# Modulation weights of a two-layer block: products and sums on VectorE, one operation a tile

## The reference, cut to what matters

```python
# x: 512 tokens x 1024 features, f32. First block: two attentions (differential, latent), gated and merged
merged = sigmoid(g_diff) * (o_diff @ w_proj_diff) + sigmoid(g_mla) * (o_mla @ w_proj_mla)
x = rms_norm(x + merged @ w_out, norm_final)
# Second block: six vectors of 1024 features, the same for all tokens, shape the two sublayers
shift1, scale1, gate1, shift2, scale2, gate2 = split(silu(cond) @ mod_w + mod_b, 6)
h = rmsnorm(x, g1) * (1 + scale1) + shift1
x = x + gate1 * hyena_mix(h)            # long convolution by spectra
h = rmsnorm(x, g2) * (1 + scale2) + shift2
x = x + gate2 * conv_ffn(h)
out = rmsnorm(x, final_g)
```

## Time and profile before

| | us |
|---|---|
| runs, median of 3 | 1062.06 (1061.97 to 1062.47) |
| profiled execution | 1061.37 |
| its span, first to last instruction | 1059.3 |
| TensorE busy | 1040.0 |
| VectorE, ScalarE, GpSimd busy | 665.7, 418.6, 543.7 |

### The profile page before, as it was taken

How to read it: one execution, slowest core, us unless ns; L and a number is a source line. 1 busy time by engine, 2 the same in 40 slices (tenths; PEclk the granted TensorE clock), 3 DMA queues, 4 the chain that set the end, 5 groups by cost and what they waited for, 6 DMA issues and landing times.

```text
span 1059.3 us, 13471 instructions
## 1 busy us (share of the span) xinstructions
PE 1040.0 (98%) x4968; PEld 856.4 (81%) x4968; DVE 665.7 (63%) x1007; ACT 418.6 (40%) x687; POOL 543.7 (51%) x401
## 2 busy tenths in 40 slices
PE   7999999999999999999999999999999999999996
PEld 5889887877877888778888888778888888888885
DVE  5663776866499765985788847386666666520503
ACT  6223547665554243644444342442323223221222
POOL 1688895999200064234444346535465545553641
PEclk9999999999999999999999999999999999999999
DMA  6446454342446922212322113303222232223222
GB/s 257 164 168 225 133 187 153 90 163 70 179 159 238 379 104 100 93 67 80 110 83 84 54 42 155 143 33 146 87 80 79 103 135 79 80 80 135 104 80 79
DMA packets 19611, 131.92 MB, mean 125 GB/s; under 512 B 3411, under 2 KB 3811, under 8 KB 13030
## 3 DMA queue, kind: packets, MB, share of 16 engines
q1 hardware_dynamic: 8784, 92.62, 23.2%
q0 software_dynamic: 6560, 27.27, 8.0%
q10 hardware_dynamic: 4214, 11.30, 2.8%
HBM read 124.90 MB, written 6.30 MB: 124 GB/s over the span
## 4 chain that ended last, share of the span: by engine, by line
PE 95%; DVE 2%; ACT 1%; DMA 1%; issue 0%; POOL 0%; SPq 0%; POOLq 0%; ACTq 0%; DVEq 0%
PE bank L505 81%; PE bank L496 7%; PE bank L511 3%; PE bank L752 1%; PE bank L746 1%; DMA x_sb<-x_in 1%; PE bank L904 1%; PE bank L741 1%; DVE arena L2178 0%; DVE arena L2181 0%; PE bank L913 0%; PE bank L753 0%; PE bank L869 0%; ACT arena L1189 0%; DVE arena L2214 0%
## 5 line engine op out<-in xcount | busy, mean ns | idle before, releaser
L1730 POOL TENSOR_TENSOR ring_parts<-ring,ring_parts 128x1024 fp32r<-128x1024 f32 x102 | 248.7, 2442 | 266.3 <-ACT ring_parts L1189 263.5
L505 PE MATMUL bank<-hT_parts,ring_parts 128*128 128x512 f32 x1344 | 339.2, 393 | 0.8 <-ACT hT_parts L1518 0.8
L1189 ACT ACTIVATE ring_parts<-ring 128x1024 fp32r<-128x1024 f32 (+2 forms) x163 | 168.6, 1043 | 383.7 <-PE bank L505 219.9
L505 PEld LDWEIGHTS bank<-hT_parts,ring_parts 128*128 128x128 f32 x1344 | 249.6, 188 | 54.7 <-ACT hT_parts L1518 2.4
L505 PE MATMUL bank<-ring_parts,hT_parts 128*128 128x512 f32 (+1 forms) x672 | 171.6, 379 | 1.0 <-POOL ring_parts L1730 0.6
L505 PE MATMUL bank<-ring_parts,arena_parts 128*128 128x512 f32 (+1 forms) x736 | 172.4, 386 | 0.0
L505 PEld LDWEIGHTS bank<-ring_parts,arena_parts 128*128 128x128 f32 x736 | 136.6, 188 | 27.9 <-DVE arena L2416 0.3
L505 PE MATMUL bank<-arena_parts,ring_parts 128*128 128x512 f32 x592 | 148.0, 391 | 0.3 <-DVE arena_parts L2285 0.3
L505 PEld LDWEIGHTS bank<-ring_parts,hT_parts 128*128 128x128 f32 x672 | 122.4, 188 | 22.8 <-POOL ring_parts L1730 1.0
L2521 DVE SCALAR_TENSOR_TENSOR arena<-bank,small,arena 128x441 f32<-128x441 f32 (+2 forms) x176 | 122.3, 695 | 24.6 <-DVE arena L2521 1.7
L505 PEld LDWEIGHTS bank<-arena_parts,ring_parts 128*128 128x128 f32 x592 | 111.0, 188 | 25.4 <-DVE arena_parts L2285 2.1
(11 more groups left out here) (223 smaller groups left out, 1100.5 us busy)
## 6 DMA issues: line engine op xcount, KB each, us to landing
ring<-weights_in SPq DMA_DIRECT2D x39, 2048.0 KB, 8.0
arena<-mod_w_in POOLq DMA_DIRECT2D x32, 512.0 KB, 4.1
arena<-mod_w_in POOLq DMA_DIRECT2D x8, 1024.0 KB, 5.5
x_sb<-x_in SPq DMA_DIRECT2D x4, 512.0 KB, 5.7
ring<-weights_in SPq DMA_DIRECT2D x4, 512.0 KB, 8.5
mod_spill<-mod_part POOLq DMA_DIRECT2D x16, 128.0 KB, 2.1
x_sb<-x_in ACTq DMA_DIRECT2D x4, 512.0 KB, 12.2
arena<-mod_spill ACTq DMA_DIRECT2D x1, 2048.0 KB, 10.6
```

The source lines that it names most:

```text
L505: ins = nc.tensor.matmul(out, l, r, start=start and n == 0, stop=stop and n == len(passes) - 1)
L1189: return nc.scalar.activation(out, in_, ACT.Copy)
L1730: return nc.gpsimd.tensor_tensor(part(low), low, part(high), ALU.subtract)
```

## The change

The weights now come transposed: a tile has 128 output features on the partitions and all 1024 inputs on the columns. silu(cond) is a row that every partition holds (`cond_row`, in the first half of `mod_g`, by a transfer that spreads it and one Silu of 128x1024 behind split 8). One `scalar_tensor_tensor` on VectorE multiplies the tile with it and adds up along the columns into one column of `modc` (`mod_tile`): 48 tiles, 48 operations. Nothing is left for TensorE to add.

- 16 early tiles stand behind splits 12 to 23, through four buffers; 28 late tiles stand two by two behind splits `FIRST_GATE+6` to `FIRST_PD+3`, and four in the first half of the merge, again with four buffers. GpSimd only issues the loads, each waiting until the tile four places earlier is used, and takes the roots in between.
- `mod_spill`, `mod_back`, `ones_sq`, `modulation` and `gate_rows` on TensorE, the copies `modg_copy` and `modg_late`, and GpSimd's products are gone. VectorE's `modulation()` (bias, then 1 + scale times the norm's gain) moves from behind `norm_x2(3)` to before `add_wo(0)`.
- The gates are written as columns to HBM (`mod_row`), with a strided transfer from ScalarE's queue behind the last `square_x2`, and read back spread over all partitions.
- `small` grows by 8 columns, `modc` and the table `minus` lie ahead of the padding.

```diff
+        minus = sb("minus", [P, 256])
+        modc = sb("modc", [P, MOD_TILES])
         sb("to_line", [P, -((nc.sbuf_base + 31) // 32 * 32) % LINE // 4])
-        mod_part = sb("mod_part", [P, 2 * MOD_POOL_COLS])
-        modc = sb("modc", [P, 4 * KD])
...
+        cond_row = mod_g[:, 0, :]
+        modw_early = [at(99, D), at(103, D), at(65, D), mod_g[:, 1, :]]
+        modw_late = [at(75, D), at(79, D), at(65, D), at(69, D)]
...
-            modulation(0)
-            gate_rows(0)
             wo_tile(0)
             wo_tile(1)
-            modulation(1)
-            gate_rows(1)
             filter_tile(0)
             wo_tile(2)
-            modulation(2)
...
             wo_tile(7)
-            gate_rows(2)
-            gate_rows(3)
-            modulation(3)
...
+            chunk_landed(pool, C_DK)
+            pool.dma_start(cond_row, cond_d.partition_broadcast(P).rearrange("p a d -> p (a d)")).then_inc(sem("cond_in"), 16)
+            for j in range(MOD_EARLY):
+                load_mod(j)
+                if j == 11:
                     latent_roots()
+            for h in range(HEADS):
+                head_roots(h)
+            wait("o_ready", HEADS)
+            load_mod(MOD_EARLY)
+            load_mod(MOD_EARLY + 1)
+            wait("pv_done", 4 * UNITS)
+            for j in range(MOD_EARLY + 2, MOD_TILES):
+                load_mod(j)
...
+                V.scalar_tensor_tensor(out=w, in0=w, scalar=1.0, in1=cond_row, op0=ALU.mult, op1=ALU.mult,
+                                       accum_out=modc[:, j:j + 1]).then_inc(sem("mod_summed"), 1)
...
+                if i >= 4:
+                    mod_tile(i - 4)
-            for p in range(16, 24):
+            for p in range(16, 20):
                 split_low(p)
+                mod_tile(p - 12)
+            for p in range(20, 24):
+                split_low(p)
+                for j in range(2):
+                    mod_tile(8 + 2 * (p - 20) + j)
...
             for p in range(FIRST_GATE + 6, FIRST_PD + 4):
                 split_low(p)
+                for j in range(2):
+                    mod_tile(MOD_EARLY + 2 * (p - FIRST_GATE - 6) + j)
                 if p in (FIRST_GATE + 8, FIRST_GATE + 9):
                     split_output(p - FIRST_GATE + UNITS - 10)
                 if p - FIRST_GATE - 7 in NET_AFTER:
                     net_layer(NET_AFTER.index(p - FIRST_GATE - 7))
-                if p - FIRST_GATE in MOD_AFTER:
-                    mod_chunk(MOD_AFTER.index(p - FIRST_GATE))
...
+            wait("gates_ready", 1)
+            act.dma_start(mod_row_d.rearrange("a (t p) -> p (a t)", p=P), modc[:, 4 * KD:MOD_TILES],
+                          allow_slow_non_contiguous=True).then_inc(sem("mod_row_out"), 16)
```

More of the change, by code:

```diff
@@ L892, in _ @@
                          [(o[0][:, k, :], o[1][:, k, :]) for k in range(HEADS)]).then_inc(sem("merge_done"), 1)
[L895 to L914, removed]
             def abs_norm(n):
@@ L1256, in _ @@
                 split_high(p)
+                if p == 8:
+                    wait("cond_in", 16)
+                    nc.scalar.activation(cond_row, cond_row, ACT.Silu).then_inc(sem("cond_ready"), 1)
             for i in range(8, 12):
@@ L1951, in net_layer @@
                 wrap(r, a, k, 0).then_inc(sem("net_angle"), 1)
-            def mod_chunk(j):
-                C = MOD_DVE_COLS
-                wait(f"modw_in{j % 2}", 16 * (MOD_POOL // 2 + j // 2 + 1))
-                acc = mod_g[:].rearrange("p a b -> p (a b)")[:, j * C:(j + 1) * C]
-                w = modw_dve[j % 2]
-                for k in range(KD):
-                    ins = V.scalar_tensor_tensor(out=acc, in0=w[:, k, :], scalar=st(CSILU + k), in1=acc, op0=ALU.mult, op1=ALU.add)
-                    if k < KD - 1:
-                        link(ins)
-                ins.then_inc(sem("mod_dve_done"), 1)
             def table(t, m, groups, halves):
@@ L2107, in split_output, with modulation @@
                 V.tensor_tensor(part(low), low, part(high), ALU.subtract).then_inc(sem("oT_low"), 1)
+            def modulation():
+                wait("mod_summed", MOD_TILES)
+                V.tensor_tensor(modc[:], modc[:], small[:, SMALL["mod_b"]], ALU.add).then_inc(sem("gates_ready"), 1)
+                wait("gates_ready", 1)
+                for s, name in enumerate(("norm_g1", "norm_g2")):
+                    c = modc[:, (2 * s + 1) * KD:(2 * s + 2) * KD]
+                    ins = V.scalar_tensor_tensor(out=c, in0=c, scalar=1.0, in1=small[:, SMALL[name]], op0=ALU.add, op1=ALU.mult)
+                ins.then_inc(sem("modc_ready"), 1)
             wait("lambda_exps", 1)
@@ L2160, in _ @@
             split_low(FIRST_WO + 3)
-            def modulation():
-                wait("modc_done", 4)
-                V.tensor_tensor(modc[:], bank[3][:, 0:4 * KD], small[:, SMALL["mod_b"]], ALU.add).then_inc(sem("modc_read"), 1)
-                wait("modc_read", 1)
-                for s, name in enumerate(("norm_g1", "norm_g2")):
-                    c = modc[:, (2 * s + 1) * KD:(2 * s + 2) * KD]
-                    ins = V.scalar_tensor_tensor(out=c, in0=c, scalar=1.0, in1=small[:, SMALL[name]], op0=ALU.add, op1=ALU.mult)
-                ins.then_inc(sem("modc_ready"), 1)
+            modulation()
             def add_abs(i):
@@ L2480, in _ @@
             wait("row_in", 16)
[L2481 to L2482 removed]
+            wait("modg_in", 16)
             link(V.tensor_tensor(row[:], row[:], mod_g[:, 0, :], ALU.mult))
```

135 lines of the change are left out of this document (39 added, 96 removed).

## The result

| | before | after |
|---|---|---|
| median | 1062.01 us | 1068.01 us (1067.43 to 1068.58) |
| ratio, 95% interval | | 1.0056 (1.0044 to 1.0068) |
| profiled execution, its span | 1061.37, 1059.3 | 1067.97, 1066.2 |

The change makes the kernel 6 us slower, where 2 us less were forecast. The page of after shows what the earlier trace rows shows of before: the busy times, and the chain by engine.

What follows compares the result with a forecast made beforehand. TensorE, busy for 98% of the span, was taken to bound the kernel; -5.4 (of 10.4 us removed) + 2.9 (latent stage) + 0.4 (gate stage) = -2.1 us from the median 1062.06 gave 1060.0 us, range 1056.5 to 1066.5.

Steps and rivals of the forecast that it cites:

- The arena's start (on its line both times): Start of the arena buffer, listed among the edits at no cost.
- the mechanism of the sum: Whole kernel: -5.4 us on TensorE, +2.9 in the latent stage, +0.4 in the gate stage, together -2.1 us.
- that case's own range: Bounds of the forecast's own case, chance 0.45: 1058.8 to 1061.5 us around 1060.0.
- Places 1 and 2: After the merge and before the second normalisation: waits hide part of the 10.4 us removed from TensorE; 5.4 us gained.
- The latent stage: 115 to 145 us: tile 12's load queues behind the latent roots, delaying VectorE and the next projection; 2.9 us lost.
- T = 1.2 us: Lower near bound for one VectorE tile operation, at which the latent stage was to lose 2.4 us.
- T = 1.3 us for a tile operation: VectorE's 48 added 128x1024 operations take 1.3 us each, near bounds 1.2 to 1.5, 62 us in all.
- the rival of twice that: VectorE's accumulator makes each tile operation twice as long, 2.4 us; +17 us, 1079 us; chance 0.13.
- The gate stage: Before net_layer(0): VectorE's added tiles use up the slack before TensorE's gate tile 5; 0.4 us lost, bounds 0 and 3.
- Late tile loads: Rival: tile loads land late before net_layer(0) and at tile 12, costing 3 to 5 us; 1063 to 1065 us; chance 0.20.
- a sign of being wrong: Tile loads: the prediction would be wrong if one took over 5.5 us.
- 3 us of waiting before the second normalisation: Between wo_tile(7) and the spectrum: 3 of the 3.4 us removed from TensorE are lost to waiting.

Runs made afterwards that it cites:

- b_arena128: Kernel before with only 128 free bytes put ahead of the arena (start 115456); 1070.61 us against 1062.06, ratio 1.0079.
- a_home: Changed kernel with the arena back at byte 115328, by leaving out eight unused columns and the padding; 1058.55 us, ratio 0.9971 to before.
- a_fill3: Changed kernel with three 128x512 f32 products that nobody reads put behind wo_tile(7); 1066.62 us, ratio 1.0041 to before.
- best: Changed kernel with arena at byte 115328, latent roots behind the issue of tile 15, three unread products behind wo_tile(7); 1055.41 us, ratio 0.9937 to before.
- b_ring128: Kernel before with 128 free bytes ahead of the ring, so ring and arena move together, away from transposed inputs and residual stream; 1075.90 us, ratio 1.0128.
- b_all128: Kernel before with 128 free bytes ahead of the first buffer, so all buffers move and keep their distances; 1061.85 us, ratio 0.9997.
- a_home_roots: a_home with GpSimd's latent roots behind the issue of tile 15 instead of between tiles 11 and 12; 1056.53 us, ratio 0.9950 to before.

## Why the prediction was wrong, step by step

- **"The arena's start (on its line both times)", an edit at no cost.** This is the step that failed. It cost 8.6 us in the kernel before (b_arena128) and 9.5 here (a_home, with about 1 us of the clock in it), on the products of the ring with the arena. I took the kernel's own pad to 128 bytes for the condition and didn't work out the address: what had held before was a distance to the ring that is a multiple of 256 bytes, and the change broke it. Without this cost the mechanism of the sum holds: a_home took 1058.55 us, against 1060.0 forecast and just below that case's own range. Of the 1.4 us that it gains beyond the forecast 2.1, the gate stage is 0.4 and the end of the kernel 0.65, which I didn't have.
- **Places 1 and 2: -5.4 us.** Right. 64.37 against 69.79 us in a_home, -5.42; in after -5.11, with slower products of wo_tile in it. Both hidden parts were measured by fillers: 1.85 and 3.44 us, against 1.65 and 3.0. Taken from the 10.38 us removed they would leave a gain of 5.1; the 0.3 us between that and 5.42 stay open.
- **The latent stage: +2.9 us.** Right, though in parts that were a little off: 3.09 in after, 2.81 in a_home, and 2.2 of that gone when the roots stand behind the loads. The first tile came in 4.27 us after the issue of its load, the four tiles with a split took 5.8, and the scalings 2.46 (I had 2.6). (The prediction's terms give 2.5 and not 2.4 us at T = 1.2.)
- **T = 1.3 us for a tile operation, and the rival of twice that.** By form, VectorE in after:

```profile
L1931 DVE SCALAR_TENSOR_TENSOR arena<-arena,mod_g 128x1024 f32<-128x1024 f32 x44 | 52.6, 1217 | 10.0 <-DMA arena<-mod_w_in 10.0
...
L1931 DVE DVE_READ_ACCUMULATOR arena<-arena,mod_g 128x1 f32 x44 | 3.5, 80 | 0.0
```

  1.22 us, and a read of the accumulator of 0.08 that overlaps with the next start; from start to start two tiles back to back lie 1.14 to 1.24 us apart. The doubled operation is out. The Trainium skill, Vector Engine (DVE) Microarchitecture Reference, section 7 (Points that are easy to get wrong), has a rule by which it would take twice as long; the trace disagrees, now for the form with an accumulator too.
- **The gate stage: +0.4 us.** Too high, and the prediction's own terms end at 300.5 and not 300.6 us. It cost nothing (in a_home 2.85 us late at the piece ahead of it, 291.43 against 288.58, and 2.84 behind, 303.53 against 300.69). In after `net_layer(0)` began at 297.25 and its sine was over at 302.68, 1.6 us before TensorE's product at 304.24.
- **Late tile loads.** Not seen. A load took 4.8 us in the median of 44 (4.1 before) and 7.2 in that of the four into `mod_g`, over the 5.5 that I had named as a sign of being wrong, but 9.7 of the 10.0 us that VectorE waited for loads were the one wait behind the roots.
- **TensorE's clock wasn't in the sum.** I counted 3 us of waiting before the second normalisation as a gain not made, and nothing more. The fall that follows takes 1.0 us of what is gained elsewhere, in the executions that have it.

## What to carry to other kernels

When an edit changes the size of anything that lies ahead of a large buffer, print the start addresses of before and after and compare the distances between the buffers that one product reads together. A pad that rounds one start says nothing of them. Here the distances tried that are multiples of 256 bytes cost nothing, and those 64 and 128 bytes beyond one cost 7.3 to 13.5 us. Second, when the removal of TensorE's work ends in a wait, look at the granted clock behind it: filler work shorter than the wait cost nothing and gave about 1 us back (a_fill3, best). Third, before reading a filler's effect, read the filler's own duration.

## What the runs showed of the hardware

A 128x512 f32 product whose two operands are in buffers that start a multiple of 256 bytes and 128 (or 64) more apart takes some 6 ns longer, of 0.2275 us from start to start. It shows with the arena as the first operand and as the second (391 to 396 and 389 to 395 ns), it follows the pair and not a buffer (b_ring128), and moving all buffers alike does nothing (b_all128). Distances of 64, 128 and 256 bytes beyond the old one were tried; why the distance counts, the runs don't show. VectorE's eight scalings took 9.78 us beside GpSimd's products and 2.46 with GpSimd idle (2.45 in a_home_roots); that GpSimd is the cause is likely and not isolated, as no run changes its work alone. In after this gained no time on TensorE, since the scalings began 11.9 us later.
